# Placing expert rows more densely on TensorE's order among the jobs of two parts of a two-layer block

## What is computed

```python
def one(xs):                       # peer(): 128 tokens at a time
    q = (xs @ wq).reshape(PEER_BLOCK, PEER_HEADS, 2, PEER_HALF)
    s1 = einsum('nhd,hkd->nhk', q[:, :, 0], keys[0]); s2 = einsum('nhd,hkd->nhk', q[:, :, 1], keys[1])
    t1, i1 = top_k(s1, 16); t2, i2 = top_k(s2, 16)
    ...                            # best 16 of the 256 sums: top, eid
    g = softmax(top, axis=-1)
    a = gelu(einsum('nd,nhjd->nhj', xs, u[eid]), approximate=False)
    return einsum('nhj,nhjd->nd', g * a, v[eid])
```

## Time and profile before

| | us |
|---|---|
| median of 3 runs | 3569.28 |
| the profiled execution | 3574.3 |
| its span, first to last instruction | 3572.3 |
| TensorE busy | 2872.3 |
| VectorE busy | 1754.3 |
| ScalarE busy | 1113.5 |
| GpSimd busy | 834.7 |
| mean granted clock of TensorE | 0.894 |

### The profile page before, as it was taken

One profiled execution on the slowest core, in us unless ns is written; L12 is line 12 of the kernel. 1 busy time (PEld: TensorE's weight loads), 2 busy tenths in 40 slices (PEclk: granted clock), 3 DMA queues, 4 the chain that ended last, 5 costly groups with the idle time before them and its releaser, 6 DMA issues.

```text
span 3572.3 us, 42719 instructions
## 1 busy us (share of the span) xinstructions
PE 2872.3 (80%) x16338; PEld 1803.2 (50%) x16338; DVE 1754.3 (49%) x4345; ACT 1113.5 (31%) x3085; POOL 834.7 (23%) x772
## 2 busy tenths in 40 slices
PE   7899998978898999988765656589999885556555
PEld 5677887644555666565411211177888751111111
DVE  1323013548676565554766667413310156667664
ACT  1322102243555444334433232232310123323232
POOL 0000000323333332312244444200000024444432
PEclk9999999989999999998877777799999997777876
DMA  8544441988998999977799999831234189999996
GB/s 327 236 187 179 153 153 57 386 320 332 363 379 314 421 420 419 379 309 278 290 412 418 399 416 414 331 118 48 94 134 152 72 339 421 418 410 415 411 405 271
DMA packets 151107, 1071.64 MB, mean 300 GB/s; under 512 B 16564, under 2 KB 18228, under 8 KB 22520
## 3 DMA queue, kind: packets, MB, share of 16 engines
q0 software_dynamic: 110592, 805.36, 55.8%
q1 hardware_dynamic: 40312, 263.56, 19.1%
HBM read 1067.80 MB, written 1.05 MB: 299 GB/s over the span
## 4 chain that ended last, share of the span: by engine, by line
PE 53%; DMA 25%; DVE 10%; ACT 7%; issue 3%; POOL 2%; DVEq 0%; ACTq 0%; SPq 0%; POOLq 0%
PE bank L374 40%; DMA ring<-in_experts,eid 25%; PE bank L388 11%; DVE ring L1319 4%; POOL ring L1740 2%; PE bank L467 1%; ACT topk_work L874 1%; ACT topk_work L867 1%; ACT topk_work L864 1%; PE bank L401 1%; ACT L864 1%; ACT h_even L927 0%; ACT L958 0%; DVE state L1506 0%; ACT scratch L915 0%
## 5 line engine op out<-in xcount | busy, mean ns | idle before, releaser
L1740 POOL DMA_INDIRECT ring<-in_experts,eid x768 | 834.5, 1087 | 2698.3 <-PE bank L388 1378.3
L388 PE MATMUL bank<-ring,topk_work 64*64 64x512 f32 x6144 | 976.8, 764 | 554.3 <-ACT topk_work L874 551.9
L1319 DVE CUSTOM_DVE_ANT_0 ring<-ring,h2tok 128x1024 f32<-128x1024 f32 x768 | 937.8, 1225 | 591.7 <-DMA ring<-in_experts,eid 588.4
L388 PEld LDWEIGHTS bank<-ring,topk_work 64*64 64x64 f32 x6144 | 235.7, 158 | 1200.3 <-ACT topk_work L874 911.7
L864 ACT ACTIVATE topk_work<-topk_work 128x2 f32<-128x2 f32 x384 | 78.0, 203 | 1164.6 <-DVE topk_work L1319 1164.0
L374 PE MATMUL bank<-h_even,weights 128*128 128x256 f32 (+1 forms) x1360 | 311.0, 387 | 18.7 <-ACT h_even L927 18.7
L374 PEld LDWEIGHTS bank<-h_even,weights 128*128 128x128 f32 (+1 forms) x1360 | 249.8, 186 | 81.8 <-issue 22.0
L374 PE MATMUL bank<-h_odd,weights 128*128 128x256 f32 (+1 forms) x1056 | 240.5, 384 | 3.6 <-DVE xT L1341 1.9
L874 ACT ACTIVATE topk_work<-const,topk_work 128x64 f32<-128x64 f32 x768 | 225.7, 341 | 0.4 <-ACT topk_work L867 0.4
L374 PEld LDWEIGHTS bank<-h_odd,weights 128*128 128x128 f32 (+1 forms) x1056 | 195.7, 188 | 57.2 <-issue 24.8
L867 ACT ACTIVATE topk_work<-topk_work 128x1 f32<-128x1 f32 x768 | 184.6, 287 | 12.6
(11 more groups left out here) (223 smaller groups left out, 3151.9 us busy)
## 6 DMA issues: line engine op xcount, KB each, us to landing
weights<-in_quads SPq DMA_DIRECT2D x150, 1024.0 KB, 8.1
ring<-in_quads SPq DMA_DIRECT2D x85, 1024.0 KB, 4.9
ring<-in_experts,eid POOLq DMA_INDIRECT x768, 9.1
ring<-in_quads SPq DMA_DIRECT2D x6, 768.0 KB, 4.2
weights<-in_quads SPq DMA_DIRECT2D x6, 768.0 KB, 6.8
weights<-in_quads SPq DMA_DIRECT2D x12, 256.0 KB
xT<-in_xT SPq DMA_DIRECT2D x1, 2048.0 KB, 10.9
out<-h_even SPq DMA_DIRECT2D x1, 1024.0 KB, 4.5
```

Source lines behind the costliest of these rows:

```text
L388: x = nc.tensor.matmul(acc[g][out, :], diag[mine, J % 4, :], ring[mine, J % RING, D + h * 512:D + (h + 1) * 512], start=first, stop=J % TI ...
L1319: v.tensor_tensor_reduce(row, row, h2tok[:, u // UNITS % 2, :], 1.0, 0.0, ALU.mult, ALU.add, dots[:, u % 2, j:j + 1]).then_inc(S["dot_done ...
L1740: pool.indirect_dma_start(ring[:, J % RING, :], None, d["experts"], bass.IndirectOffsetOnAxis(eid[:, u % 2, j:j + 1], 0)).then_inc(gathere ...
```

## The change

A constant `PACE` of 1.0 is added to the modelled time of every job from the first quarter of the queries of pass 1 until the jobs of pass 2 are written; so the plan believes that more time passes between jobs and places more pairs. And behind the sums of squares of pass 2's first norm `breathe(8.0)` is called.

```diff
+PACE = 1.0
 ...
-            cur = {"q": None, "slots": (), "turn": 0, "next": 0, "limit": 0, "pass": 0}
+            cur = {"q": None, "slots": (), "turn": 0, "next": 0, "limit": 0, "pass": 0, "pace": 0.0}
 ...
                 full_now[key] = plan.now
-                plan.now += 0.1
+                plan.now += 0.1 + cur["pace"]
 ...
                         if q == 1 and 2 * g * UNITS in LEADS:
                             plan.first_rows()
+                            cur["pace"] = PACE if g == 1 else 0.0
 ...
                 if n != 1:
                     square_sums("norm1", n, DC)
+                if n == 2:
+                    breathe(8.0)
 ...
                 else:
+                    cur["pace"] = 0.0
                     rows_until(first_pair(p.beside + 1))
                     tile_sum(2 * p.beside + 1)
```

## The result

The changed kernel takes 3546.53 us (median of 5 runs, 3543.77 to 3554.81), the one before 3569.95 us beside it (5 runs). The ratio is 0.9932, with a 95% interval of 0.9916 to 0.9948: 24 us faster, 19 to 30. The forecast was 3552, a gain of 17: inside the range on record, and just short of the measured interval. The profiled execution took 3546.53 us with a span of 3544.5; before it was 3574.3.

What follows compares the result with a forecast made beforehand. DMA engines bound group 1's tail, so their idle time ahead of it counts: 16.8 + 4 + 8 + 4 + 6 + 13.8 = 52.6 against 69.8 us, a gain of 17.2; forecast 3552 us, range 3524 to 3575.

Steps and rivals of the forecast that it cites:

- the tail: Group 1's last pairs, at the DMA engines' rate: 133.1 us shorter, about 374 us in place of 502.
- E: Gates, 1660 to 1680: a pair cuts the gap into two of about 9 us, bridgeable; idle 6 us for 9.0.
- B: 1540 to 1600: five pairs come in; DMA engines idle 4 us, for 3.6 before.
- C: Sums of squares, 1600 to 1620: two pairs behind them recover 4.8 us, leaving 8 us idle of 12.8.
- D: 1620 to 1660, behind the sums of squares: four pairs come in; idle 4 us, for 4.8 before.
- F: Linear attention and what follows, 1680 to 1800: twelve pairs come in, share 0.92 for 0.81, idle 13.8 us for 22.8.
- A: 1500 to 1540, norm of pass 1 and choice of first experts: ahead of the pace, idle time kept at 16.8 us.
- Table loads: Two more on ScalarE: 2.6 us by the row, held in the shares; 5.3 by the skill page, forecast then 3555.
- Rival 1: From 1500 to the tail the DMA share does not rise: idle 83.8 us, slower, 3583 us; chance 0.12.
- Rival 2: Ahead of the tail idle time only moves: sum 66.8 us, gain 3 us, 3566, nothing measurable; chance 0.16.
- Rival 3: DMA engines never rest behind 1540 but for C: idle 22.8 us, gain 47, 3522 us; chance 0.12.
- Rival 4: Weights come late, more rows in flight delaying quads: no time cost by itself; counted within the forecast, no separate chance.

Runs made afterwards that it cites:

- e1: The changed kernel without breathe(8.0) behind the sums of squares of pass 2, 24 of 26 pairs still moved: ratio 0.9961 to the kernel before.
- e2: The changed kernel with PACE = 0.0, so breathe(8.0) alone, 2 pairs moved: ratio 0.9982 to the kernel before.
- e6: The changed kernel with a plain copy in place of gelu for pairs 124 to 255: ratio 0.9912 to the kernel before.
- e7: The changed kernel with ScalarE's work on the gates in two groups of two: ratio 0.9883 to the kernel before.
- e11: The changed kernel with pace 1.5 and breathe in pass 2 alone, and the gates in twos: ratio 0.9932 to the kernel before.
- e10: The changed kernel with pace and breathe in pass 2 alone, and the gates in twos: 3538.18 us, ratio 0.9882 to the kernel before.
- e8: The changed kernel with a pace of 0.5 also from the queries of pass 0 to those of pass 1: 3646.35 us, ratio 1.021.

## Why the prediction was right

The mechanism was the one forecast: work of the DMA engines moved ahead of the tail fills their idle time, and the tail shortens by all of it. Tail 371 us for the 374 forecast (the forecast's own difference, 502 less 133, is 369), its start at 1905 for 1916, share before it 0.89 for 0.87. That 52.6 us of idle time came so near the measured sum is luck in part: E and the tail were too small by 8 us together, B, C, D and F too large by 11, and most of that cancels.

- A (to 1540): 16.8, as forecast.
- B (queries): 1.5 idle for 4. The right bound was a full share.
- C and D (norm and first products): 12 forecast, 6.3 measured, from 17.6. This is the term with the wrong size. I counted only what the two pairs let in during the norm; e1 and e2 show that they act behind it. The price was wrong too: not 2.6 us on the path to the first product but 8.5 (20.3 for 11.8; in e2, with one pair, 5.7), since the product stands behind a pair whose share on ScalarE begins only when the shift is done. It stayed hidden: the DMA engines rest only 2.4 us in the stretch behind.
- E (gates): 6 forecast, 10.0 measured. The pair in the middle cut GpSimd's wait only to 12.91 us: the pair stands behind two gates on ScalarE and its dot products behind the second gate on VectorE, and GpSimd had no free slot until TensorE used it. The step that said gaps of 9 us could be bridged failed. e6 and e7 show a cause of half of it, the table loads; the chain over VectorE (4.07 us) is read from the trace and not tested.
- F (linear attention): 13.8 forecast, 11.1 measured; the share came to 0.93, the upper of the two rows of pass 1.
- The tail was to have no idle time; its window shows 0.99, 3.7 us. That is rounding for the most part: in windows of 5 us it is 2.2 us, and 2.3 before, so the change did nothing to it.
- Table loads: the Trainium skill, ScalarE: Activation LUTs, section "What ACT_TABLE_LOAD costs", adds a drain of 1380 ns to each switch. The rows of the gates show none: a load that starts at 1699.55 and takes 1.28 us is followed by an activation at 1700.85, and it follows one that ends at 1699.53. The price of one switch by the row was the right one.
- Sum: 52.6 forecast, 49.4 measured, 17.2 against 20.7 us won; in windows of 5 us, 47 left and 24 to 25 won, and 24 in the runs.

Rival 1, the share that does not rise, fell: F went from 0.79 to 0.93. But denser is not always better: e11 has more idle time than e10, and in e8 TensorE waits for its pairs. Rival 2 had one half right, the gates. Rival 3 asked too much, 22.8 us of idle time for the 47 measured. Rival 4 did not show: from 1500 to the tail no wait for weights is in the changed kernel's trace.

## What to carry to other kernels

Where one resource bounds a stretch, add up its idle time ahead of it: with the start and the same work, it gave the end of the tail within 2 us in eleven kernels and within 6 in the twelfth, whatever else was moved. Ask whether a stretch that the same resource bounds follows; in pass 1, with none behind it, an edit of the same kind made the changed kernel 2.8% slower. Read a long stretch in short windows: a share that is rounded to 0.01 can hide some us of idle time over 500 us. A pair placed in front of a wait pays behind the wait, by the slots it frees.

## What the runs showed of the hardware

On ScalarE more than half of a gate's 4.5 us are its two table loads, and taking the gates in twos, 6.2 us for two in place of 9.0, was worth more (0.58% alone, 0.5% on top of the change) than expected: 17 loads of 1.28 us fewer in the whole kernel, 22 us of ScalarE's time, brought 21 and 17 us. It was also not expected that a denser order could cost TensorE 60 us more of waiting at nearly the same DMA share, 0.90 for 0.92 (e8).
